# A two-block decoder on one core: the first stage (gated linear attention) reordered

## The reference, cut to what matters

```python
hn = x * rsqrt(mean(x * x) + 1e-5) * gain
q, k, v, r, lr_f, lr_b = split(hn @ w_in)          # 512, 512, 1024, 1024, 16, 16 columns
q = q * 128 ** -0.5                                # 4 heads: 128 wide for q and k, 256 for v
log_a = log_sigmoid(lr @ wg + bg) / 16             # one for each direction
# in each direction, chunks of 64 tokens: decay inside a chunk, and a state carried across:
state = state * exp(b_last)[..., None] + upd       # upd = (k * exp(b_last - b)).T @ v
o = o_intra + (q * exp(b)) @ state_before_chunk    # both directions are added
o = o * rsqrt(mean(o * o) + 1e-5) * head_gain      # per head, over its 256 columns
h = x + (o * silu(r)) @ w_out
```

## Time and profile before

| | |
|---|---|
| time, 3 executions | 1728.27 us median (1726.26 to 1728.9) |
| the profiled execution, first to last instruction | 1727.5 us |
| PE, DVE, ACT busy | 94%, 71%, 60% of it |
| mean granted TensorE clock | 0.974 |
| the stage of the change | first instruction to about 172 us |

### The profile page before, as it was taken

How to read it: one execution, slowest core, us unless ns; L and a number is a source line. 1 busy time by engine, 2 the same in 40 slices (tenths; PEclk the granted TensorE clock), 3 DMA queues, 4 the chain that set the end, 5 groups by cost and what they waited for, 6 DMA issues and landing times.

```text
span 1727.5 us, 21544 instructions
## 1 busy us (share of the span) xinstructions
PE 1619.7 (94%) x8649; PEld 1358.3 (79%) x8649; DVE 1227.4 (71%) x1298; ACT 1036.3 (60%) x1244; POOL 60.0 (3%) x62
## 2 busy tenths in 40 slices
PE   5999999987979999999999999999998989889987
PEld 5877788887768788888888888888877877688866
DVE  3655555458558888888888888888885566555665
ACT  4644544355557767777776776777676446454463
POOL 0000000012100000000000000000000200003000
PEclk9999999998979999999999999999998999899999
DMA  7422555552239999999999999999897533246410
GB/s 250 147 98 91 189 184 178 188 204 80 99 120 328 398 314 361 333 351 369 333 332 321 395 338 345 331 327 392 307 338 181 111 109 97 50 86 136 125 46 37
DMA packets 133081, 389.31 MB, mean 225 GB/s; under 512 B 8695, under 2 KB 14267, under 8 KB 132845
## 3 DMA queue, kind: packets, MB, share of 16 engines
q1 hardware_dynamic: 132692, 387.15, 65.9%
q10 hardware_dynamic: 280, 0.69, 0.1%
HBM read 386.77 MB, written 1.05 MB: 224 GB/s over the span
## 4 chain that ended last, share of the span: by engine, by line
PE 80%; DVE 9%; ACT 7%; issue 3%; DMA 0%; ACTq 0%; DVEq 0%; POOL 0%
PE psum L356 25%; PE psum L358 24%; PE psum L357 24%; DVE wlo L189 4%; ACT whi L179 3%; PE psum L1533 1%; PE psum L1585 1%; DVE Ss L1229 1%; DVE mx L1234 1%; PE psum L2252 1%; ACT hh L1645 0%; PE psum L2097 0%; PE psum L2238 0%; PE psum L2143 0%; PE psum L1614 0%
## 5 line engine op out<-in xcount | busy, mean ns | idle before, releaser
L189 DVE TENSOR_TENSOR wlo<-raw,whi 128x2048 fp32r<-128x2048 f32 (+1 forms) x286 | 628.4, 2208 | 223.7 <-ACT whi L179 223.0
L179 ACT ACTIVATE whi<-raw 128x2048 fp32r<-128x2048 f32 (+1 forms) x286 | 525.8, 1847 | 237.1 <-PE psum L358 237.1
L356 PE MATMUL psum<-whi,xh 128*128 128x512 f32 (+1 forms) x1280 | 497.5, 389 | 18.3 <-DVE xl L2598 9.9
L358 PE MATMUL psum<-whi,xl 128*128 128x512 f32 (+1 forms) x1280 | 485.6, 379 | 0.0
L357 PE MATMUL psum<-wlo,xh 128*128 128x512 f32 (+1 forms) x1280 | 484.9, 379 | 0.0
L356 PEld LDWEIGHTS psum<-whi,xh 128*128 128x128 f32 x1280 | 242.2, 189 | 75.2 <-issue 13.4
L358 PEld LDWEIGHTS psum<-whi,xl 128*128 128x128 f32 x1280 | 241.9, 189 | 49.5
L357 PEld LDWEIGHTS psum<-wlo,xh 128*128 128x128 f32 x1280 | 242.6, 190 | 45.6 <-issue 0.2
L189 DVE TENSOR_TENSOR wlo<-raw_more,whi 128x2048 fp32r<-128x2048 f32 (+1 forms) x94 | 204.1, 2177 | 39.5 <-ACT whi L179 38.9
L179 ACT ACTIVATE whi<-raw_more 128x2048 fp32r<-128x2048 f32 (+1 forms) x94 | 171.4, 1827 | 53.8 <-PE psum L358 53.8
L356 PE MATMUL psum<-xh,whi 128*128 128x256 f32 (+2 forms) x552 | 165.3, 299 | 16.8 <-DVE wlo L189 15.2
(11 more groups left out here) (363 smaller groups left out, 1515.9 us busy)
## 6 DMA issues: line engine op xcount, KB each, us to landing
raw<-in_moe_w_down_dram SPq DMA_DIRECT2D x58, 1024.0 KB, 7.8
raw<-in_moe_w_gate_dram SPq DMA_DIRECT2D x43, 1024.0 KB, 6.2
raw<-in_moe_w_up_dram SPq DMA_DIRECT2D x41, 1024.0 KB, 5.9
raw_more<-in_moe_w_down_dram SPq DMA_DIRECT2D x30, 1024.0 KB, 7.7
raw<-in_w_in_dram SPq DMA_DIRECT2D x28, 1024.0 KB, 8.0
raw_more<-in_moe_w_up_dram SPq DMA_DIRECT2D x23, 1024.0 KB, 5.2
raw_more<-in_moe_w_gate_dram SPq DMA_DIRECT2D x21, 1024.0 KB, 6.2
raw<-in_moe_w_up_dram SPq DMA_DIRECT2D x23, 768.0 KB, 5.5
```

What stands on the lines that cost most here:

```text
L179: act.e.activation(self.whi[:, i % self.ns, 0:kt * n], self.place[self.slots[i]][:, 0:kt * n], ACT.Copy, scale=1.0).then_inc(self.s_hi)
L189: dve.e.tensor_tensor(self.wlo[:, i % self.ns, 0:kt * n], self.place[self.slots[i]][:, 0:kt * n], self.whi[:, i % self.ns, 0:kt * n].bitca ...
L356: pe.e.matmul(o, lh, rh, start=start, stop=False)
L358: return pe.e.matmul(o, ll, rh, start=False, stop=stop)
```

## The change

The first weight matrix (q) is cut into pieces of 1, 1, 2 and 4 groups of 128 rows instead of 4 and 4. The small rows other than the first gain move from ACT's queue to SP's, behind the first four pieces and the rest of the constants; ACT's queue fetches only the first gain and the 128 columns of the identity. x is fetched in halves by columns. PE transposes x itself, not the scaled x; q is multiplied in k-major order as the groups come; the norm's factor is multiplied into q, k and lr (by DVE, from a tile `rb` that holds it along the free axis) and into v and r (by ACT, as `scale`). The gate products come after the first quarter of "vr0". "vr3" is cut by tokens: one half stays, the other (`r_tile(pe, 0, ...)`) comes behind the states. A state step takes both directions of two heads, alternating between them, and the states alternate between two tiles. The head norm's root is a power on POOL. The turn of o and "gla out0" are interleaved. Its core:

```diff
-    add_k("gla q", gw, 0, 512)
+    P["gla q"] = 0
+    for k, kt in ((0, 1), (1, 1), (2, 2), (4, 4)):
+        pieces.append((gw.rearrange("(k p) n -> p k n", p=128)[:, k:k + kt, 0:512], kt, 512))
...
     class Start:
         def sp(sp):
-            for t in range(2):
-                sp.e.dma_start(H[:, t, :], I["x"][0, t * 128:(t + 1) * 128, :]).then_inc(ld_x, 16)
-            sp.wait_ge((ld_prm, 16 * len(rows)))
+            for half in range(2):
+                c = slice(half * 512, half * 512 + 512)
+                sp.e.dma_start(H[:, :, c], I["x"][0, :, c].rearrange("(t p) c -> p t c", p=128)).then_inc(ld_x[half], 16)
             for i in range(RAW):
                 W.fetch(sp, i)
+            sp.e.dma_start(cst[:, 128:W1], I["c1"][:, 128:W1]).then_inc(ld_c1, 16)
+
         def act(act):
-            act.e.dma_start(cst[:, :], I["c1"]).then_inc(ld_c1, 16)
-            for at, r in zip(pcol, rows):
-                act.wait_ge((s_prm0, 1))
-                act.e.dma_start(prm[at:at + r.shape[0], :], r).then_inc(ld_prm, 16)
-            act.wait_ge((s_prmT, 1))
-            act.e.activation(pc[:, :], psum[:, 0, 0:72], ACT.Copy, scale=1.0).then_inc(s_pc)
+            act.e.dma_start(prm[0:8, :], rows[0]).then_inc(ld_first, 16)
+            act.e.dma_start(ident, I["c1"][:, 0:128]).then_inc(ld_first, 16)
+            act.wait_ge(s_set.at("one"))
+            act.e.activation(st[:, 44:45], st[:, 45:46], ACT.Sqrt, bias=0.0, scale=1.0)
...
+            for k in range(4):
+                turned(k)
+            for k in range(8):
+                q(k)
+                if k < 4:
+                    turned(k + 4, x(k))
+            pe.wait_ge(x(6))
+            Start.pe_params(pe)
+            pe.wait_ge(n_dve.at("gla", "rstd"), x(7))
+            for j in range(2):
+                ins = pe.e.matmul(psum[:, 7, j * 128:(j + 1) * 128], st[:, j:j + 1].to_broadcast([128, 128]), ident, start=True,
+                                  stop=True)
+            ins.then_inc(s_prmT.end("rstd"))
+            run(standing_steps(pe, "gla k", G4, [4, 5, 6, 7], T, x, [[x(4)], [x(5)], [s_pc.at("rest")], [s_pc.at("rstd")]]))
             run(standing_steps(pe, "gla lr", [(0, 128)], [0], T, x, [[q_out.at(0)]], 1))
+            vr0 = moving_steps(pe, "gla vr0", [0, 128], [1, 2], x, [[q_out.at(1)], [q_out.at(2)]])
+            next(vr0)
             for i, (d, j) in enumerate(DJ):
                 b = [5, 6, 7, 0][i]
-                pe.wait_ge((s_one, 1), (ld_wg, 64), (lr_out, 1) if b == 0 else k_out.at(b - 4))
+                pe.wait_ge(s_set.at("lr"), (ld_wg, 64), (lr_out, 1), k_out.at(b - 4 if b else 3))
                 pe.e.matmul(psum[:, b, :], lrT[:, j * 128:(j + 1) * 128], wg[:, d, :], start=True,
                             stop=True).then_inc(z_acc.end(i))
-            run(moving_steps(pe, "gla vr0", [0, 128], [1, 2], x, [[q_out.at(1)], [q_out.at(2)]]))
+            run(vr0)
+            pe.wait_ge((ld_c1, 16))
             for d in range(2):
                 tri, bk = (c1("trif"), [5, 6]) if d == 0 else (c1("trib"), [7, 0])
...
+            def grow(s, hp):
+                if s:
+                    pe.wait_ge(S_at(s - 1, 0, hp), S_at(s - 1, 1, hp))
+                else:
+                    pe.wait_ge(klN_out.at(1, 1), sc_out.at(1, hp), v_at)
+                for h in (2 * hp, 2 * hp + 1):
+                    for d in range(2):
+                        c = s if d == 0 else 3 - s
+                        pp, j = (c % 2) * 64, c // 2
+                        ins = pe.e.matmul(psum[:, GB[d][hp], (h % 2) * 256:(h % 2) * 256 + 256],
+                                          klN[pp:pp + 64, d, j, h * 128:(h + 1) * 128], v[pp:pp + 64, j, h * 256:(h + 1) * 256],
+                                          start=True, stop=True)
+                ins.then_inc(grown.end(s, hp))
+
+            def cross(s, hp):
+                pe.wait_ge(S_at(s, 0, hp), S_at(s, 1, hp), *qb_at[0], *qb_at[1])
+                for h in (2 * hp, 2 * hp + 1):
+                    for d in range(2):
+                        nx = s + 1 if d == 0 else 2 - s
+                        op, oj = (nx % 2) * 64, nx // 2
+                        ins = pe.e.matmul(o_at(oj, h)[op:op + 64, :], qb[:, d, h * T + nx * 64:h * T + nx * 64 + 64],
+                                          states[s % 2][:, d, h * 256:(h + 1) * 256], start=False, stop=True,
+                                          skip_group_check=True)
+                ins.then_inc(crossed.end(s, hp))
+
...
-                    ins.then_inc(crossed.end(s, d))
+                for hp in range(2):
                     if s < 2:
-                        grow(s + 1, d)
-            free = {2: [og_out.at(3)], 3: [og_out.at(5)], 4: [og_out.at(7)], 5: [S_out.at(2, 0)], 6: [S_out.at(2, 0)],
-                    7: [S_out.at(2, 1)]}
-            turn(pe, "gla out", [(og[:, j, :], 128, j * 128) for j in range(2)], [[og_out.at(1)], [og_out.at(3)]], free, OB)
+                        grow(s + 1, hp)
+                    cross(s, hp)
+            run(r_tile(pe, 0, 0, S_at(2, 1, 1)))
             y = x_is("gla out")
-            run(moving_steps(pe, "gla out0", [0, 128], [0, 1], y, [[S_out.at(2, 1)], [og_out.at(1)]]))
-            out1 = moving_steps(pe, "gla out1", [0, 128], [4, 5], y, [[y(4)], [y(6)]])
+
+            def turned_out(k):
+                pe.wait_ge(og_out.at(3 if k > 3 else 1), [S_at(2, 0, 0), S_at(2, 0, 1), S_at(2, 1, 0), og_out.at(5), y(1), y(2), y(3),
+                                                          og_out.at(3)][k])
+                for j in range(2):
+                    ins = pe.e.transpose(psum[:, OB[k], j * 128:(j + 1) * 128], og[:, j, k * 128:(k + 1) * 128], ident)
+                ins.then_inc(s_turn.end("gla out", k))
+
+            for k in range(4):
+                turned_out(k)
+            out0 = moving_steps(pe, "gla out0", [0, 128], [0, 1], y, [[r_out.at(1, 0)], [og_out.at(1)]], fine=True)
+            run(islice(out0, 6))
+            for k in range(4, 8):
+                turned_out(k)
+            run(out0)
+            out1 = moving_steps(pe, "gla out1", [0, 128], [4, 5], y, [[og_out.at(7)], [y(0)]])
             next(out1)
             next(out1)
             for k in range(4):
@@ -694,18 +800,23 @@
             run(out1)
```

ACT's and DVE's programs at the start, and the head norm on POOL:

```diff
+            def high(k):
+                act.wait_ge(s_turn.at("gla", k), s_pc.at("gain"))
+                act.e.activation(xh[:, k, 0:T], psum[:, 4 + k % 4, 0:T], ACT.Identity, bias=0.0,
+                                 scale=pc[:, G_MIX[0] + k:G_MIX[0] + k + 1]).then_inc(s_xhi.end("gla", k))
+
+            for k in range(4):
+                high(k)
+                W.hi_to(act, k)
+            high(4)
+            high(5)
+            W.hi_to(act, 4)
+            high(6)
+            high(7)
+            squares(act, "gla", 0, [(H[:, j, :], 128) for j in range(2)], v[:, :, :].rearrange("p a b -> p (a b)"), (ld_x[0], 16),
+                    (ld_x[1], 16))
             root(act, "gla", st[:, 0:2])
...
+            for hp in range(2):
+                c = head_cols(hp)
+                pool.wait_ge(hn_sq.at(hp))
+                pool.e.tensor_scalar(c, c, 1e-5, None, ALU.add).then_inc(hn_eps.end(hp))
+                pool.wait_ge(hn_eps.at(hp), s_set.at("power"))
+                pool.e.tensor_tensor(c, c, power[:, :].to_broadcast([128, 4]), ALU.pow).then_inc(hn.end(hp))
...
+            def low(k):
+                dve.wait_ge(s_xhi.at("gla", k))
+                dve.e.scalar_tensor_tensor(xl[:, k, 0:T], psum[:, 4 + k % 4, 0:T], pc[:, G_MIX[0] + k:G_MIX[0] + k + 1],
+                                           xh[:, k, 0:T].bitcast(F32), ALU.mult, ALU.subtract).then_inc(s_xlo.end("gla", k))
+
+            for k in range(4):
+                low(k)
+                W.lo_to(dve, k)
+            low(4)
+            low(5)
+            W.lo_to(dve, 4)
+            low(6)
+            low(7)
             mean(dve, "gla", st[:, 0:2], D, 1e-5)
             invert(dve, "gla", st[:, 0:2])
-            scaled_dve(dve, "gla", xn)
-            low_by_gain(dve, "gla", T, G_MIX[0])
-            W.lo_to(dve, P["gla k"] + 1 + NS)
+            W.lo_to(dve, P["gla k"] + 2)
+            Start.dve_params(dve)
+            dve.wait_ge(s_prmT.at("rstd"))
+            dve.e.tensor_copy(rb[:, :], psum[:, 7, 0:T]).then_inc(s_pc.end("rstd"))
+            for h, mark in enumerate(done("gla q", 4, 4)):
+                dve.wait_ge(mark, s_pc.at("rstd"))
+                dve.e.scalar_tensor_tensor(qT[:, h, :], psum[:, h, 0:T], float(128 ** -0.5), rb[:, :], ALU.mult,
+                                           ALU.mult).then_inc(q_out.end(h))
+            W.lo_to(dve, P["gla lr"] + 2)
             for h, mark in enumerate(done("gla k", 4)):
                 dve.wait_ge(mark)
-                dve.e.tensor_copy(kT[:, h, :], psum[:, 4 + h, 0:T]).then_inc(k_out.end(h))
+                dve.e.tensor_tensor(kT[:, h, :], psum[:, 4 + h, 0:T], rb[:, :], ALU.mult).then_inc(k_out.end(h))
```

(38 more changed lines are left out.)

253 lines of the change are left out of this document (143 added, 110 removed).

## The result

The changed kernel took 1703.83 us (median of 4 runs, 1702.98 to 1704.47), the kernel before 1727.91 us on the same chip (4 runs, 1726.26 to 1728.9): ratio 0.9859, 95% interval 0.9847 to 0.9871, so 22 to 26 us less. Its profiled execution took 1702.98 us, with a span of 1701.2 against 1727.5, 26.3 us shorter. The forecast was 1704.1.

The account below looks back on a forecast made before the run. PE, busy 94% of the span, was taken as the bound; gains of 8.6 (start), 0.8 (z) and 14.75 ("vr3" to "gla out0"), 24.2 us off span 1727.5, gave 1703.3, so 1704.1 us; own range 1700 to 1707.

Parts of the forecast that it names:

- the start: From the kernel's begin to k: q starts at 7.75, k at 26.9 instead of 35.55; gain 8.6 us, ends 6 to 10.
- the wait inside q: Before q's group 3, PE idles 3.1 us for weight piece 3, converted by ACT behind split 5, then by DVE.
- DVE holding k: At k's start, PE is ready at 25.8 but waits until 26.9 for DVE to end k's first weight piece.
- z: Before z, the 0.83 us wait goes, as its work moves beside 2.8 us of "vr0"; gain 0.8 us.
- the state blocks: State chain: twelve blocks take 13.6 us, grows 1.16 and crosses 1.11 each, 0.1 us of each grow added for changing shape.
- "vr3" to "out0": From "vr3" to "gla out0": 47.4 us before, 32.75 after, adjusted for turn and clock; gain 14.75 us, ends 9 to 16.
- The head norm's idle: Behind the last cross: 3.68 us idle goes, 4.9 us of norm covered by 6.6 us of PE work; 0.75 remains.
- the half clock behind it: Behind the head norm, 139 to 144.7 us: slow clock goes, gaining 1.8 us on the turn and 1.0 on "out0".
- (1): State crosses: column halves do not overlap, 4.6 us less gain, 1708.7 us; chance 0.25.
- (2): q's groups 3 to 7 stay at half clock after PE's idle, costing 5.8 less 1.1 us, 1708.8 us; chance 0.10.
- (3): Experts wait on their weights, so the gain does not reach the end, 1728 us; chance 0.02.
- (4): Later stages: PE's idles shift against clock changes; 48 us more half clock loses 24 us, with 60, 1734; chance 0.03.

Follow-up runs that it names:

- Experiment 5: Changed kernel with q's weights in two pieces of four groups instead of pieces of 1, 1, 2 and 4: 1703.98 us, single execution.
- Experiment 8: Changed kernel with identity fetched ahead of x, last projection's weights converted earlier, and q's fourth piece cut in two: 1700.94 us, ratio 0.9839.
- experiment 6: Changed kernel with ACT's first copy and DVE's two remainders of "vr3" weights made earlier, among the gated-key work: 1700.05 us, single execution.
- experiment 2: Changed kernel with both halves of "vr3" ahead of the states, so nothing covers the head norm: 1708.03 us, ratio 0.9885.
- experiment 3: Changed kernel up to "vr2" only; "vr3" order, states, head norm and turn of o as in the kernel before: 1716.99 us, ratio 0.9938.
- the second run of the kernel after: Changed kernel run again with nothing changed, beside the one with three edits on the same chip: 1704.55 us, ratio 0.986.
- experiment 1: Changed kernel with grow and cross products issued direction by direction instead of alternating: 1700.28 us once, then 1702.81 us, ratio 0.986, timed several times.
- experiment 4: Changed kernel with weight pieces issued only once x, the identity and the first gain have landed: 1703.91 us, single execution.
- experiment 9: The kernel with three edits, plus ring pieces before remaining constants, k's first piece converted before the squares, norm spread behind k's first group: 1698.39 us, ratio 0.9831.
- experiment 7: Changed kernel with the identity fetched on SP's queue ahead of x instead of on ACT's beside it: 1702.43 us, single execution.

## Why the prediction was right, and where it was not

**The sum.** 24.2 us were forecast; 24.1 came by the medians and 26.3 by the profiled executions. In every run that has both on record the time is 1.8 to 2.0 above the span, where I had added 0.8. By that the profiled execution of the kernel before, 1727.5, stands for about 1729.3 (an estimate), more than any of its four times, while that of the kernel after was the fastest of its four. So the traces show a gain about 2 us larger than is usual, and that the median came within 0.3 us of the forecast is in part luck: spans of the same kernel differ by 2 us (1701.2 and 1703.1) with the start and with the later clock. The mechanisms were those named but for two in the start, the place of the wait inside q and DVE holding k; three terms were mis-sized: the start, z a little, and the state blocks.

**The start: 8.6 forecast, 10.1 measured** (9.0 when the kernel ran again). There are three errors. The start of k before was taken as 35.55 and was 35.09, which made the term 0.5 too large. I had the identity and x at 4.4; PE was released by the identity at 5.62, and q started at 8.82 instead of 7.75. And the step "PE idle of about 3 before group 3, ended by DVE's piece 3" was wrong: pieces are of 1, 1, 2 and 4 groups, so the third holds groups 2 and 3, and the fourth is wanted first by group 4. PE turns the last group of x at 16.86, before it waits, so ACT has the last split done at 17.75 and not at 20.0, and starts the squares at 17.65. The wait was 1.53 instead of 3.1, and DVE ended k's first two pieces at 26.7 with PE already in k: its first product, at 25.02, has no wait, where 26.9, held by DVE, was forecast. That is 1.9 us; less the 0.5, the term was 1.4 too small. Experiment 5 shows how much hangs on the pieces. Experiment 8 shows how close the norm's chain stands behind PE: with PE 2.2 us earlier at the end of q, k is held by DVE as in the forecast.

**z: 0.8 forecast, 1.0 measured.** The sums came 11.1 earlier and k 10.1, and z starts with no wait; 0.83 of it is the wait of the earlier trace rows. The wait before "vr3" stayed, 1.66, as said; experiment 6 shows it was a matter of ACT's and DVE's order.

**"vr3" to "out0": 14.75 forecast, 15.5 measured** (26.6 less 11.1). The twelve blocks took 12.15 (94.31 to 108.39, less 1.93 for the products inside the last chunk) instead of 13.6, against 22.4 before. The 0.1 us that I had added to a grow for the change of shape and the 0.1 in a cross, taken over from the rows, were too much: 1.06 and 1.02 instead of 1.16 and 1.11. And five blocks stand next to one of their own shape and took less still: two grows 1.93, three crosses 2.93. DVE was not late. The head norm's idle fell from 3.68 to 0.83 (0.75 forecast), and the half clock behind it went, 2.8 us forecast. From the measured parts: 10.25 + 2.85 + 2.8 = 15.9, 0.4 more than the measured sum; experiment 2 measures the last two together as 4.8 to 5.1 where I had 5.7. The 2.8 held for the one profiled execution of the kernel before, with its 6.8 us at half clock; with the 3.4 us of experiments 2 and 3 it is 1.7.

On the crosses the Trainium skill ("TensorEngine Tiling (Array Packing)", Key Properties) has tiles that run loads and products in parallel. The trace agrees: eight instructions of the two column halves last 1.08, eight of one alone 1.94.

**The rivals.** (1) Column halves do not overlap: refuted by the rows of L764. (2) The start stays at half clock: refuted, a product takes 0.28 from 12.6 us on. In the second run of the kernel after this came at 14.4, which with q's later start (9.17) makes the 1.07 us between the two at k. (3) The gain does not reach the end: refuted, span and marker moved alike. (4) The later clock: its stretches moved with the work (before they began at 363.2 and 407.5, after at 336.7 and 381.1), and half-clock time went from 93.3 to 86.5 us, the missing 6.8 being those behind the head norm. The luck of plus or minus 3 us is there (experiment 1), but nothing near 48 us.

**Open.** Why a stretch at half clock behind 330 us is there in one execution and missing in another, and what sets the moment at which the clock rises in q. What the early fetch alone is worth at k (experiment 4). What each edit of experiment 9 is worth alone. Of the parts of the change that have no run of their own (x turned before its norm, the gate products behind the first quarter of "vr0", the power on POOL) only the traces speak.

## What to carry to other kernels

Where weights come in pieces, write down which group stands in which piece and what PE does before it needs one, before costing a wait: the wait is between two such events, not at the head of a loop. Small products that fill half the rows or half the output columns are worth issuing beside those of the other half, and a chain of small norm steps is worth a projection beside it, since the idle costs twice, as time and as clock. Compare kernels at a marker of the work behind the change; here the span alone could be off by 3 us.

## What the runs showed of the hardware

- Column halves of fp32 products (64 output columns each, at two places of the array) run side by side as fully as row halves do: pairs of them start 6 to 7 ns apart, and four products take 1.02 us instead of 1.87.
- The order in which the halves are queued does not matter within eight instructions (experiment 1: 1.07 and 1.02). Across halves, instructions do not start in the order of the program: in the kernel before, the first instruction of the second direction's grow starts at 113.89, and the last of the first direction's eight, which stand ahead of it, at 114.53.
- A DMA of 64 KB on a second queue beside x's 1 MB landed at 5.6 to 6.3 us; ahead of x on the same queue at 2.7 (experiment 7).
- In this stage, idle of 3.7 to 3.8 us at full clock was each time followed by half clock: for 3.4 us, beginning 0.9 and 1.2 us after PE had gone on, in two kernels (experiments 3 and 2), and for 6.8 in the kernel before, beginning within the idle. Idle of 1.4 to 1.7 us at full clock never was.
